# A hybrid mixer and expert layer on one core: gathers and projections moved across two stage seams, arguments and keys of the scans moved to ACT, masks to GpSimd

## What is computed

```python
h = rms_norm(x, g_norm1) * (1 + sc1) + sh1
bg, cg, xg, qg, kg, vg, og, igr, fgr = split(h @ w_in)
conv = bg * conv3(cg * xg)                       # per grid row of 64
# each head, direction and chunk of the scan:
dmat = where(tril, b[t] - b[s] + i[s], -inf)
s = (q @ k.T) * exp(dmat - m_t)
num = a * (q @ C) + s @ v
C_new = decay * C + (w_s * k).T @ v
h = num / maximum(abs(den), exp(-m_t))           # both directions added, normed, * sigmoid(og)
x = x + ga1 * (concat(conv, h) @ w_out)
# PEER, for each token: e = 16 of 128 x 128 pairs of keys, for 8 heads
w = softmax(score) * gelu(xb . u_tab[e])
x = x + ga2 * sum(w * v_tab[e])
y = rms_norm(x, g_final)
```

## Time and profile before

| | us |
|---|---|
| median of 3 runs | 3586.84 (3585.72 to 3594.46) |
| the profiled execution | 3596.01 |
| its span, first to last instruction | 3594.3 |
| PE busy in it | 3003.1 (84%) |
| DVE busy | 2539.0 (71%) |
| POOL busy | 1523.6 (42%) |
| ACT busy | 911.1 (25%) |

### The profile page before, as it was taken

The page is one execution under the profiler, slowest core; times in us unless marked ns, Lnnn a source line. Parts: engine busy times, 40 slices in busy tenths (PEclk is TensorE's granted clock), DMA queues, the critical chain, the costliest instruction groups (busy, mean ns, idle before and its releaser), DMA issues.

```text
span 3594.3 us, 33409 instructions
## 1 busy us (share of the span) xinstructions
PE 3003.1 (84%) x10068; PEld 1526.5 (42%) x10068; DVE 2539.0 (71%) x6056; ACT 911.1 (25%) x2291; POOL 1523.6 (42%) x1301
## 2 busy tenths in 40 slices
PE   6986979896488888898888888888888888888887
PEld 4753434443244434444443444344434434443443
DVE  3457777784766777777777767777777777677765
ACT  1211111111122323222233223223222232232222
POOL 0003565340444544454444444444444444444442
PEclk8987989897799999999999999999999999999999
DMA  8555787675999999999999999999999999999998
GB/s 354 178 157 191 244 306 276 226 285 197 364 416 413 407 420 419 408 408 417 408 408 416 416 412 409 413 418 411 415 406 413 395 419 415 411 401 420 420 412 339
DMA packets 227809, 1317.53 MB, mean 367 GB/s; under 512 B 24688, under 2 KB 44592, under 8 KB 95024
## 3 DMA queue, kind: packets, MB, share of 16 engines
q0 software_dynamic: 184320, 1208.04, 83.2%
q1 hardware_dynamic: 43312, 107.36, 8.1%
HBM read 1305.29 MB, written 10.01 MB: 366 GB/s over the span
## 4 chain that ended last, share of the span: by engine, by line
DVE 31%; PE 20%; DMA 15%; issue 3%; ACT 3%; DVEq 2%; POOL 1%; POOLq 0%
PE acc L1507 15%; DMA room<-in_uv,expert 15%; DVE room L1745 15%; PE mix L1473 3%; PE ps_q L1451 2%; DVE wt L1658 2%; ACT gelu L1564 2%; DVE work L1642 1%; DVE work L1638 1%; DVE picked L1645 1%; DVE ind L1606 1%; DVE ind L1599 1%; DVE pos L1626 1%; ACT diag L1570 1%; DVE work L1600 1%
## 5 line engine op out<-in xcount | busy, mean ns | idle before, releaser
L1507 PE MATMUL acc<-room,diag 128*128 128x512 f32 x4096 | 1947.2, 625 | 389.7 <-ACT diag L1570 389.5
L1437 POOL DMA_INDIRECT room<-in_uv,expert x1024 | 1232.3, 1203 | 1400.2 <-PE acc L1507 1198.2
L1745 DVE CUSTOM_DVE_ANT_0 room<-room,h 128x1024 f32<-128x1024 f32 x1024 | 1230.4, 1221 | 364.8 <-DMA room<-in_uv,expert 362.4
L1507 PEld LDWEIGHTS acc<-room,diag 128*128 128x128 f32 x4096 | 784.0, 199 | 1454.1 <-issue 1453.6
L1570 ACT ACTIVATE diag<-ident,wt 128x128 f32<-128x128 f32 x1024 | 377.4, 397 | 505.7 <-PE acc L1507 399.0
L1564 ACT ACTIVATE gelu<-dot 128x2 f32<-128x2 f32 x512 | 104.4, 204 | 1220.8 <-DVE dot L1745 1219.7
L1009 PE MATMUL region<-hT_then_w_out,w 128*128 128x512 f32 x800 | 368.6, 622 | 38.8 <-DVE seen L1196 32.5
L997 POOL DMA_INDIRECT room<-in_uv,cexpert x235 | 267.0, 1136 | 234.8 <-DVE acc L1182 123.0
L1658 DVE SCALAR_TENSOR_TENSOR wt<-gelu,rz,ex 128x2 f32<-128x2 f32 x512 | 113.6, 222 | 268.3 <-ACT gelu L1564 268.3
L1009 PEld LDWEIGHTS region<-hT_then_w_out,w 128*128 128x128 f32 x800 | 158.8, 201 | 240.4 <-issue 240.4
L1451 PEld LDWEIGHTS ps_q<-h2T,wq 128*128 128x128 f32 x2048 | 243.2, 195 | 40.4 <-issue 31.2
(11 more groups left out here) (301 smaller groups left out, 1997.4 us busy)
## 6 DMA issues: line engine op xcount, KB each, us to landing
w<-in_w_in SPq DMA_DIRECT2D x49, 512.0 KB, 5.1
room<-in_w_ada SPq DMA_DIRECT2D x12, 2048.0 KB, 17.3
room<-in_uv,expert POOLq DMA_INDIRECT x1024, 11.4
room<-in_wq SPq DMA_DIRECT2D x8, 1024.0 KB, 6.9
wq<-in_wq SPq DMA_DIRECT2D x1, 7168.0 KB, 29.3
xt<-in_x SPq DMA_DIRECT2D x9, 512.0 KB, 19.2
out_y<-x SPq DMA_DIRECT2D x9, 512.0 KB, 8.4
room<-in_w_out SPq DMA_DIRECT2D x2, 2048.0 KB, 12.0
```

Of the source, the lines that this page charges most:

```text
L1437: nc.gpsimd.indirect_dma_start(out=uv[:, k % RING, :], out_offset=None, in_=t["uv"], in_offset=bass.IndirectOffsetOnAxis(ap=expert[:, h % ...
L1507: last = nc.tensor.matmul(acc[i % 2][:, a * BANK:(a + 1) * BANK], diag[:, k % DIAG, :], uv[:, k % RING, D + a * BANK:D + (a + 1) * BANK], ...
L1745: last = nc.vector.tensor_tensor_reduce(out=uv[:, k % RING, 0:D], in0=uv[:, k % RING, 0:D], in1=h2[:], scale=1.0, scalar=0.0, op0=ALU.mult ...
```

## The change

1. PE makes two more projections at the end of the context's stage: og and cg of head 0 (project_first(3, OG), project_first(4, CG)). ACT evicts them into `og0` and `cg0`, in front of the exponential of the last query head. The mixer leaves both out in head 0; the count of jobs and of evictions is now made from a list (ELSEWHERE, JOBS).
2. GpSimd gathers the first four context rows at the end of the context's stage, when its outputs are stored and the first head's experts are chosen. The ring's slots are in another order, so that these four fall into free parts of `room`.
3. arguments(d) leaves DVE. ACT makes relu(col - offset) from PSUM, eight instructions, then exp(-x), then the weighted keys, eight scaled copies. The context's `cols` are stored with the opposite sign for this, in two instructions in place of one.
4. The masks leave DVE. GpSimd selects from the scores `sT` once for each direction and head (into `sT_back` and in place), behind the gather of the 22nd row of the head. DVE's weights(d) keeps the copy of the decays and two products.
5. BESIDE becomes 22, 5, 7, ... in place of 16, 7, 7, ...: 69 rows a head and 38 in the last, 245 in all. GpSimd gathers 8 rows beyond these in the mixer. In the expert stage BESIDE_MIX is 10: DVE does ten of the 11 rows that are left before it waits for the modulation's vectors, and one behind the first choice.

The diff, cut to its core:

```diff
+                pool.wait_ge(state_out, 16 * 12)
+                pool.wait_ge(chosen, 1)
+                for k in range(cx["early"]):
+                    nc.gpsimd.indirect_dma_start(
+                        out=cx["ring"][k], out_offset=None, in_=t["uv_rows"],
+                        in_offset=bass.IndirectOffsetOnAxis(ap=expert[:, 0, k:k + 1], axis=0),
+                    ).then_inc(cx["rows_in"][k], 16)
...
+                project_first(3, OG)
+                project_first(4, CG)
...
-                nc.scalar.copy(cols[:].rearrange("p a b c h -> p (a b c h)"), ps_cols[:, 0:16 * NT])\
-                    .then_inc(cols_ready, 1)
+                by_kind = ps_cols[:, 0:16 * NT].rearrange("p (a b n) -> p a b n", a=2, b=2)
+                flat_cols = cols[:].rearrange("p a b c h -> p a b (c h)")
+                nc.scalar.activation(flat_cols[:, :, 0], by_kind[:, :, 0], ACT.Copy, scale=-1.0)
+                nc.scalar.copy(flat_cols[:, :, 1], by_kind[:, :, 1]).then_inc(cols_ready, 1)
...
+                act.wait_ge(q_done, 5)
+                act.wait_ge(first_done, 4)
+                nc.scalar.activation(og0, pp[1][:], ACT.Sigmoid).then_inc(first_taken, 1)
+                act.wait_ge(first_done, 5)
+                nc.scalar.copy(cg0, pp[0][:]).then_inc(first_taken, 1)
                 soften(PH - 1)
...
-                                                       ALU.add, ALU.min)
+                                                       ALU.subtract, ALU.min)
...
+ELSEWHERE = {(0, "og"), (0, "cg")} | {(HEADS - 1, name) for name in HANDED_ON}
+JOBS = [(h, name) for h in range(HEADS) for name in BODY if (h, name) not in ELSEWHERE]
...
-    BESIDE = ((16, 7, 7, 4, 4, 3, 7, 4, 15), (16, 7, 7, 4, 4, 3, 7, 13, 6), (16, 7, 7, 4, 4, 3, 7, 4, 15),
-              (16, 7, 7, 4))
+    BESIDE = ((22, 5, 7, 4, 4, 3, 7, 4, 13), (22, 5, 7, 4, 4, 3, 7, 7, 10), (22, 5, 7, 4, 4, 3, 7, 4, 13),
+              (22, 5, 7, 4))
+    MASK_AFTER = 22
...
+        sT_back = sb("sT_back", [P, NL, P])
...
+        cx["begun"] = min(PICKS + V_PICKS + RS, 2 * PICKS)
...
-                for k in range(PICKS + V_PICKS):
+                starts = [sum(map(sum, BESIDE[:h])) for h in range(HEADS)]
+                for k in range(cx["early"], cx["begun"]):
+                    if k - MASK_AFTER in starts:
+                        wait_evicted(pool, starts.index(k - MASK_AFTER), "s")
+                        nc.gpsimd.affine_select(out=sT_back[:], in_=sT, compare_op=ALU.is_ge, fill=0.0, base=0,
+                                                pattern=[[0, NL], [-1, P]], channel_multiplier=1)
+                        pool.drain()
+                        nc.gpsimd.affine_select(out=sT, in_=sT, compare_op=ALU.is_ge, fill=0.0, base=0,
+                                                pattern=[[0, NL], [1, P]], channel_multiplier=-1).then_inc(masked, 1)
...
-                    project_own("og")
+                    if h:
+                        project_own("og")
...
-                    project_own("cg")
+                    if h:
+                        project_own("cg")
...
-                        wait_evicted(act, h, f"u{d}")
-                        nc.scalar.activation(seen[:], seen[:], ACT.Exp).then_inc(exped, 1)
+                        act.wait_ge(jobs_done, job_done(h, f"u{d}"))
+                        for c in range(NL):
+                            last = nc.scalar.activation(seen[:, c, :], tiles(f"u{d}")[:, c], ACT.Relu, scale=-1.0,
+                                                        bias=cols[:, d, 0, c + 1, h:h + 1])
+                        last.then_inc(free[region_of(f"u{d}")], 1)
+                        act.drain()
+                        nc.scalar.activation(seen[:], seen[:], ACT.Exp, scale=-1.0)
+                        act.drain()
+                        end = P - 1 if d == 0 else 0
+                        for c in range(NL):
+                            last = nc.scalar.activation(kw[:, c, :], ktok[:, c, :], ACT.Copy,
+                                                        scale=seen[:, c, end:end + 1])
+                        last.then_inc(weighted, 1)
                         evict(f"a{d}", qa, tiles(f"a{d}"))
...
-                    def arguments(d):
-
-                        dve.wait_ge(jobs_done, job_done(h, f"u{d}"))
-                        for c in range(NL):
-                            last = nc.vector.tensor_scalar(seen[:, c, :], tiles(f"u{d}")[:, c],
-                                                           cols[:, d, 0, c + 1, h:h + 1], 0.0, ALU.add, ALU.min)
-                        last.then_inc(free[region_of(f"u{d}")], 1)
...
                         end = P - 1 if d == 0 else 0
-
-                        dve.wait_ge(exped, h * 2 + (d + 1))
-                        wait_evicted(dve, h, "ktok")
+                        if d == 0:
+                            dve.wait_ge(masked, h + 1)
+                        dve.wait_ge(weighted, h * 2 + (d + 1))
                         wait_evicted(dve, h, f"a{d}")
                         nc.vector.tensor_copy(dec[:], qa[:, :, end])
-                        nc.vector.tensor_tensor(kw, ktok, seen[:, :, end:end + 1].to_broadcast([P, NL, P]),
-                                                ALU.mult).then_inc(weighted, 1)
                         dve.drain()
                         nc.vector.tensor_tensor(qa, qa, by_tile(qT[:]), ALU.mult)
-                        nc.vector.tensor_tensor(seen[:], seen[:],
-                                                masks[:, d, :].unsqueeze(1).to_broadcast([P, NL, P]), ALU.mult)
-                        dve.drain()
-                        nc.vector.tensor_tensor(seen[:], seen[:], sT, ALU.mult).then_inc(ready, 1)
+                        nc.vector.tensor_tensor(seen[:], seen[:], sT_back[:] if d else sT, ALU.mult).then_inc(ready, 1)
...
-    BESIDE_MIX, BESIDE_QUERY = 0, 0
+    BESIDE_MIX, BESIDE_QUERY = 10, 0
...
-                for k in range(PICKS + cx["v_done"], 2 * PICKS):
+                for k in range(cx["begun"], 2 * PICKS):
...
-            cx = {"ring": [rows[:, r] for r in (4, 5, 6, 7, 8, 9, 13, 14)], "slots": 8, "spare": [rows[:, r] for r in (0, 1, 2, 3, 10, 11, 12)],
+            cx = {"ring": [rows[:, r] for r in (8, 9, 13, 14, 4, 5, 6, 7)], "slots": 8, "early": 4, "spare": [rows[:, r] for r in (0, 1, 2, 3, 10, 11, 12)],
```

35 lines of the change are left out of this document (17 added, 18 removed).

## The result

The changed kernel takes **3544.7 us** (median of 4 runs, 3542.9 to 3546.9), the kernel before beside it 3586.5 (4 runs). The ratio is **0.988** (95%: 0.986 to 0.989). I had 3519 with a range of 3504 to 3546: the sign held, the range held by 1.3 us, and the likeliest value was 26 us too low. The profiled execution of the new kernel has a span of 3545.1 us, that of before 3594.3, so the traces differ by 49.2 us and the medians by 41.8; the profiled execution of before (3596.0) lay 9.5 us above this median of 3586.5 and the new one 2.1 above its own.

The account below looks back on a forecast made before the run. DMA bounds the expert stage for 2650 us, so everything is decided before 944 us, where PE and DVE wait in turn. Mixer 44.2 (50.4 less 6.2) plus seam 24.1 gives 68.3 us off the 3586.8 median: 3519 us, range 3504 to 3546.

Parts of the forecast that it names:

- The context's end: Before the mixer: two projections joining PE's queue make the mixer start 6.2 us later, at 311.7.
- Head 0's k at 380.4: In the mixer's head 0, PE's k starts near 380.4 us, 13.7 us earlier into the stage than before.
- Masks on GpSimd: In each mixer head: selects of 1.1 us each, 2.5 us a pair with the drain, without DVE waiting for them.
- 11 us a pair: Slow mask selects in the mixer: each head waits some 6 us, 24 in all, giving 3543 us; chance 0.05.
- Rival (a): Rows starve mixer heads 0 and 1 at 1.6 us a row, each losing 8 us: 3535 us; chance 0.25.
- Gathers at 2 us: Sign of being wrong: gathers in mixer heads 0 and 1 stay at 2 us.
- (b): PE keeps its full clock for the mixer's decay and k, last rows not starved: 12 us more, 3507; chance 0.13.
- (c): Only the seams pay, DVE's row order sets a head's length: 3555 us; chance 0.07.
- (d): Slower: GpSimd's 128x1024 select runs many times over 1.1 us; at 30 us a pair 3607 us; chance 0.03.
- Keys on ACT: In the mixer: eight scaled copies cost about 2.2 us against DVE's 1.22, hidden behind cg in heads 1 to 3.
- Head 3, 4.5: Last mixer head: kv of d = 1 moves from 73.2 to 68.5 us, a gain of 4.5 us.
- The expert seam, 24.1: Mixer to expert stage: ten rows fill DVE's wait, third 1 MB gather's row lands at 58.0 instead of 82.1: gain 24.1 us.

Follow-up runs that it names:

- e5: The changed kernel with og and cg of head 0 projected inside the mixer again, early gathers left in: 3545.2 us, ratio 0.987.
- e13: The kernel of e9 with og and cg of head 0 projected inside the mixer again: 3505.0 us, ratio 0.977.
- e1: The changed kernel with GpSimd's second select written into y's buffer and the drain between the two selects removed: 3537.1 us, ratio 0.985.
- e2: The changed kernel with the mask products back on DVE and no selects on GpSimd: 3527.3 us, ratio 0.984.
- e3: The kernel before with only a GpSimd drain added in front of the gather of each head's 23rd row: 3588.9 us, ratio 1.000.
- e10: The kernel of e1 (masks on GpSimd, no drain between selects) with the row table of e9: 3513.0 us, ratio 0.979.
- e7: The kernel of e2 with each head's first stretch of rows 16 long again instead of 22: 3546.9 us, ratio 0.988.
- e9: The kernel of e2 with rows moved from before the first division to where DVE waits for PE: 3511.0 us, ratio 0.978.
- the square above: Four kernels with masks on DVE; arguments and keys on ACT: 3527.3 us (22 rows first), 3546.9 (16); on DVE: 3583.2 (22), 3576.7 (16).
- e11: The kernel of e9 with ACT evicting the decays before its key copies and DVE taking them before waiting for keys: 3513.6 us, ratio 0.979.

## Why the prediction was right in sign and range, and wrong in size

**The context's end, +6.2:** right (6.5), and so were its parts: second projection's copy at 308.6, table load at 309.7. What e5 and e13 add: this price bought nothing. My sum gave head 0 7.0 us more gain than head 1, with PE early there for want of og and cg. The traces have 6.6 more, but e5 has them with both projections back in head 0, so that the difference came out by luck (it may be that of the one execution of the kernel before, see the sum below); head 0 was set by DVE's rows.

**Head 0's k at 380.4:** it came at 385.6, 5.2 late. DVE came to its copy of the decays in time (347.7, where I had 348.4); the five rows behind it, not gathered during the drain, put it 3.3 us late at the chain (359.9 against 356.6), and 5 at the denominators. From k on, the rest of head 0 took 67.2 us, where I had 66.8 (135.5 - 68.7).

**Masks on GpSimd, "2.5 us a pair with the drain":** this is the step that failed, a term that was mis-sized. The selects were well sized from the two small ones (1.1; measured 1.1 to 1.5), and the drain was given nothing: GpSimd's own work was done, and I had no row of a drain behind gathers. With it a pair takes 9.2 us (338.55 to 347.70). I had listed 11 us a pair as a case of its own, at 3543 us, with a chance of 0.05. The time came near it, but in part by luck: that case had DVE wait 6 us a head for the masks, 24 in all, and it waited 5.0 in all; the rest was lost on rows that came late. The claim that GpSimd issues the 22nd gather 8 us ahead of DVE was near the truth, and the drain used those 8 us up. e1, e2 and e3 show it: 7.7 us for the drain and 17 (14 by the ratios) for the masks' place as a whole. My sum had a gain there, the 9.8 us of the two products a head that DVE no longer does. With these back on DVE the same sum gives 3529, an estimate from the prediction and e2's rows, and e2, which is that kernel, took 3527.3: in the total the masks' place covers the whole miss, though head by head the sum and e2 differ (138, 139 and 136 against 132.8, 134.5 and 138.5). e10 adds a condition: the place costs this much only while DVE, and not PE, sets the heads.

**Rival (a), starved rows:** partly true and tied to the masks. Row waits in heads 0 and 1 are 15.5 and 9.8 us in the kernel before, 14.2 and 10.4 in the changed one and 7.6 and 6.1 in e2. "Gathers at 2 us" was to be a sign of being wrong: 42 of the 142 gathers in these heads took 1.6 us or more, where it had been 44 of 142, so that sign stood; e2, nearly at the forecast, still has 37 of 142. The rule that I quoted there (the Trainium skill, SBUF — State Buffer, Who interferes with whom: a DVE instruction with two SBUF inputs contends with a GpSimd one that reads SBUF) agrees with one more row: a select takes 2.07 us beside DVE's dot products (e1, head 0) and 1.09 in heads 2 and 3, where DVE's rows go to an accumulator in PSUM. The dot product beside the changed kernel's first select took 1.98 us instead of 1.23.

**Rivals (b) to (d):** (b) did not come: PE's rows of decay in head 0 took 3.78 us and k 16.6. The mixer gained 23.3 us where (c) had 8; its premise, that DVE's order of rows sets a head's length, is what e5, e7 and e9 bear out. (d) is out with selects of 1.1 to 1.5 us.

**Keys on ACT:** 2.45 us instead of 2.2, hidden behind cg as forecast. The arguments were even (2.2 us on either engine), so against the rule that relu belongs to VectorE (the Trainium skill, ScalarE: Activation LUTs, Rules for kernel authors, which gives VectorE's speed in bf16 as the reason; here all is float32) the move paid. With the masks on DVE it was worth more than either seam: by the square above 7.4 us a head with 16 rows first and 14 with 22, where DVE's instructions and its wait for the exponential come to 11 (2 x (2.15 + 1.22 + 2.13)).

**Head 3, 4.5** (73.2 - 68.5 would be 4.7): nothing came. I moved kv of d = 1 up with the arguments and left out that without a k projection ACT's chain of relu, exponential, keys and eviction stands bare: DVE waits 5.3 us, and kv comes 4.4 us later than I had it. Turning ACT's order round (e11) did not bring it back.

**The expert seam, 24.1:** 20.8. Mix ran 17.0 us instead of 15.5 (15.4 in e1 and e2 and 17.0 in e13, so it varies from run to run) and the choice ended 2 us later for it; the first two expert rows landed 4.7 us apart instead of 2.6. Mechanism as forecast.

**Sum.** Mixer 23.3 instead of 44.2 (-20.9), seam -3.3, run-to-run difference in the expert loop +5.0; that gives the 49.2 us between the traces. 7.4 us of them are there because the profiled execution of before lay 9.5 us above its median and the new one 2.1. Some of it is in head 0: in the trace of e3, the kernel before with four drains more, that head took 150.3 us and not 155.1 (heads 1 and 2: 150.2 and 147.3), so the 14.4 us of gain in the table may hold up to 5 us that are the one execution's.

## What to carry to other kernels

Before you put compute with a drain on the queue that issues gathers, ask what is in flight on it, and give the second instruction a buffer of its own, so that it needs no drain. An instruction moved to another engine and the work that covers it there are one edit; price and test them together: here the move without its cover brought 30 us and with it 56, and the cover without the move nothing. When a head is short of its sum, look for the place where one engine works ahead of what another waits for, and move filler work from there to where the first one waits: here a table of numbers was worth 16 us.

## What the runs showed of the hardware that I had not expected

- A drain on GpSimd takes 6 to 10 us with row gathers of 0.5 MB under way, with nothing else ahead of it (8.5 us in head 0 of e3_drain_alone), and 0.1 us with none (at 87.7 us in the changed kernel); the profile calls it "issue". It outlasts the transfers: the rings are empty 1.2 us before it ends in head 0 of the changed kernel and 3.8 us before in head 1 of e3.
- A select of 128x1024 takes 1.09 us, and 1.4 to 2.07 beside DVE's back-to-back dot products. The gathers' issue goes from 0.94 to 1.98 us beside dot products that start 1.15 us apart, and stays at 0.97 where they start 1.28 apart (e2, head 1).
- Taking 64 of 377 matmuls from head 0 (e13 to e9) took 25 us of PE's busy time but only 3 of its length; the mean granted clock of the stretch fell from 0.93 to 0.84, and 16 matmuls of the key-value product took 3.78 us at 0.50 instead of 1.95 at 1.00.
